# A hybrid diffusion layer on one Trainium2 core: the order of the input projection, its modulation tiles and its recurrent part

## The reference

```
mod = silu(cond) @ w_mod + b_mod          # 6 x 2048: shift, scale, gate for mixer and FFN
h = rmsnorm(x, g0) * (1 + sc_m) + sh_m
u = h @ w_in                              # 5120 columns, 10 blocks of 512
   aq ak av | bx bg | cq ck cv | dq dk dv
o_a = diff_attention(rope(aq), rope(ak), av)        # 4 heads
o_b = scan_fwd + scan_bwd of the gated bx, times gelu(bg)   # recurrent part (RG-LRU), 4 x 128 channels
o_c = neighbourhood attention (context: plain)      # 4 heads
o_d = gqa(rope(rmsnorm(dq)), rope(rmsnorm(dk)), dv) # 4 query heads, 2 key heads
x = x + g_m * rmsnorm([o_a o_b o_c o_d] @ w_out, g1)
x = x + g_f * rmsnorm((silu(g) * a) @ w_ffn_out, g3)
```

## Time and profile before

| | before |
|---|---|
| time, median of 3 | 1951.66 us (1950.04 to 1957.4) |
| the profiled execution: time, span | 1952.1 us, 1950.3 us |
| mean granted TensorE clock | 0.968 |
| PE busy | 1810.2 us (93%), 9305 matmul records |
| PEld busy | 1538.0 us (79%) |
| DVE busy | 828.4 us (42%) |
| ACT busy | 652.4 us (33%) |
| POOL busy | 138.7 us (7%) |
| DMA | 315.20 MB, mean 162 GB/s |

### The profile page before, as it was taken

The page is one execution under the profiler, slowest core; times in us unless marked ns, Lnnn a source line. Parts: engine busy times, 40 slices in busy tenths (PEclk is TensorE's granted clock), DMA queues, the critical chain, the costliest instruction groups (busy, mean ns, idle before and its releaser), DMA issues.

```text
span 1950.3 us, 21901 instructions
## 1 busy us (share of the span) xinstructions
PE 1810.2 (93%) x9305; PEld 1538.0 (79%) x9305; DVE 828.4 (42%) x1156; ACT 652.4 (33%) x915; POOL 138.7 (7%) x224
## 2 busy tenths in 40 slices
PE   5789999999866899599999999999999999999995
PEld 1457767676544788499999999999999988888884
DVE  2323445352575443553333333333333355555553
ACT  1222323243455233332222222222222334444441
POOL 1000023100283000000000000000000000000000
PEclk9899999999889899799999999999999999999998
DMA  9785777877800333133333333333333333333321
GB/s 352 310 317 217 291 296 288 307 296 292 289 1 6 116 121 130 44 129 119 122 128 130 130 130 130 120 121 127 130 130 130 130 108 126 121 122 128 130 87 65
DMA packets 44506, 315.20 MB, mean 162 GB/s; under 512 B 5388, under 2 KB 5768, under 8 KB 7096
## 3 DMA queue, kind: packets, MB, share of 16 engines
q1 hardware_dynamic: 41216, 297.95, 41.4%
q0 software_dynamic: 2864, 12.64, 1.8%
q10 hardware_dynamic: 328, 3.21, 0.5%
HBM read 308.40 MB, written 5.37 MB: 161 GB/s over the span
## 4 chain that ended last, share of the span: by engine, by line
PE 88%; POOL 4%; DVE 3%; DMA 2%; ACT 2%; issue 1%; SPq 0%; DVEq 0%; ACTq 0%; POOLq 0%
PE ps L785 38%; PE ps L580 14%; PE ps L581 14%; PE ps L582 14%; PE ps L555 4%; DMA raw<-in_weights 1%; DVE wlo L846 1%; PE ps L764 1%; POOL pool_t L1220 1%; DMA nabias<-rpb_pad 1%; PE ps L629 1%; DVE x_sb L1139 1%; ACT whi L292 1%; PE ps L607 1%; PE ps L564 0%
## 5 line engine op out<-in xcount | busy, mean ns | idle before, releaser
L846 DVE TENSOR_TENSOR wlo<-raw,whi 128x1024 fp32r<-128x1024 f32 x376 | 458.2, 1230 | 878.1 <-ACT whi L292 877.9
L292 ACT ACTIVATE whi<-raw 128x1024 fp32r<-128x1024 f32 x376 | 392.8, 1058 | 891.0 <-PE ps L785 505.4
L785 PE MATMUL ps<-h_hi,whi 128*128 128x384 f32 x1408 | 471.6, 335 | 0.0
L785 PE MATMUL ps<-h_lo,whi 128*128 128x384 f32 x1408 | 470.5, 334 | 0.0
L785 PE MATMUL ps<-h_hi,wlo 128*128 128x384 f32 x1408 | 470.4, 334 | 0.0
L580 PE MATMUL ps<-whi,h_hi 128*128 128x512 f32 x672 | 275.6, 410 | 18.7 <-DVE wlo L846 17.5
L581 PE MATMUL ps<-whi,h_lo 128*128 128x512 f32 x672 | 266.3, 396 | 0.0
L582 PE MATMUL ps<-wlo,h_hi 128*128 128x512 f32 x672 | 265.7, 395 | 0.0
L785 PEld LDWEIGHTS ps<-h_hi,whi 128*128 128x128 f32 x1408 | 264.5, 188 | 0.1
L785 PEld LDWEIGHTS ps<-h_lo,whi 128*128 128x128 f32 x1408 | 264.5, 188 | 0.0
L785 PEld LDWEIGHTS ps<-h_hi,wlo 128*128 128x128 f32 x1408 | 264.5, 188 | 0.0
(11 more groups left out here) (207 smaller groups left out, 1141.9 us busy)
## 6 DMA issues: line engine op xcount, KB each, us to landing
raw<-in_weights SPq DMA_DIRECT2D x284, 1024.0 KB, 4.9
xT<-in_x_t ACTq DMA_DIRECT2D x1, 3072.0 KB, 11.7
out<-x_sb POOLq DMA_DIRECT2D x3, 1024.0 KB, 4.7
x_sb<-in_x_sample POOLq DMA_DIRECT2D x1, 2048.0 KB, 9.6
gw<-in_lru_gate_w POOLq DMA_DIRECT2D x4, 256.0 KB, 7.5
out<-U POOLq DMA_DIRECT2D x4, 256.0 KB, 9.2
nabias<-rpb_pad POOLq DMA_DIRECT2D x16, 64.0 KB, 9.5
x_sb<-in_x_prompt POOLq DMA_DIRECT2D x1, 1024.0 KB, 5.3
```

The source lines that it names most:

```text
L292: nc.scalar.activation(whi[:, 2 * (g % RING) + b], raw[:, t % RAW, HK * b:HK * b + HK].rearrange("p k n -> p (k n)"), ACT.Copy).then_inc(w ...
L785: return nc.tensor.matmul(ps[bank][:, 0:T], w[:, k % KH * P:(k % KH + 1) * P], xs[:, k, :], start=first, stop=last)
L846: V.tensor_tensor(wlo[:, 2 * (t % RAW) + b], raw[:, t % RAW, HK * b:HK * b + HK].rearrange("p k n -> p (k n)"), whi[:, 2 * (g % RING) + b] ...
```

## The change

The blocks of the projection get another order (BX, BG, DQ, DK and DV, then AQ, AK, AV, CQ, CK, CV). Its 40 tiles become 40 steps, each with two modulation tiles ahead of one projection tile. In the first 16 steps the first four blocks take turns, one K part (four k) each; every part is a sum of its own in PSUM (bank sets 0 to 2 and 4 to 6 by turns), written to U by ACT for the first part (`part_out`) and added to U by DVE for the other three (`part_add`). From step 16 on a block's four tiles are summed in banks 0 to 2 and copied by `u_out`. Modulation uses bank 3 (and 7 for odd m below 8); m = 22 and 23 come after the last step. Within a projection tile the token block is the outer loop, and mod_turn stands behind the first token block. The recurrent part uses banks 4 to 7, begins after step 15, takes three steps per group, and PE transposes straight out of U, so the two POOL copies go. U is stored as [partition, block, token block, 512]. The input h is formed in xT instead of xnT. On POOL the norm of dq and dk moves behind the gelu of group 0, their rope behind that of group 1, and the rope of heads A behind group 3.

```diff
 def in_step(s):
+    return (s % EARLY, s // EARLY) if s < EARLY * KG else (s // KG, s % KG)
 def tile_plan():
-    for g in range(1, 4):
-        for part in range(2):
-            plan += [("mod", 2 * g + part, kg) for kg in range(KG)] + [("in", part, g - 1)]
-    plan += [("in", n, 3) for n in range(2)]
-    for e in range(N_EL):
-        m = 8 + 2 * e
-        for kg in range(KG):
-            plan += [("in", 2 + e, kg), ("mod", m + kg // 2, 2 * (kg % 2)), ("mod", m + kg // 2, 2 * (kg % 2) + 1)]
+    for s in range(STEPS):
+        m, half = 2 + s // 2, s % 2
+        plan += [("mod", m, 2 * half), ("mod", m, 2 * half + 1), ("in",) + in_step(s)]
+    plan += [("mod", m, kg) for m in (22, 23) for kg in range(KG)]
...
 # ACT
+            for s in range(STEPS):
+                if s % 2:
+                    rows_out(2 + s // 2)
+                if s + 1 < STEPS:
+                    hi("in", *in_step(s + 1))
+                if s == EARLY * KG:
+                    act.wait_ge(l_setup, 2)
+                if s < EARLY:
+                    part_out(s)
+                elif s >= EARLY * KG and s % KG == 0 and s // KG > EARLY:
+                    u_out(s // KG - 1)
+                if s % 4 == 3 and s < 12:
+                    h_high(range(s + 1, s + 5), 0, xT)
+                if lru and phase == 0:
+                    lru_in(i)          # copies, then wait l_g1(i + 1), tanh of the gelu
+                if lru and phase == 1:
+                    lru_gates(i)
+                if lru and phase == 2:
+                    lru_sqrt(i)
...
 # PE
+            def in_freed(s, tb):
+                if s < EARLY * KG:
+                    e = s - 2
+                    if e < 0:
+                        return
+                    if e < EARLY:
+                        pe.wait_ge(part_a, TB * e + tb + 1)
+                    else:
+                        pe.wait_ge(part_d, TB * (e - EARLY) + tb + 1)
+                elif s == EARLY * KG:
+                    pe.wait_ge(part_d, TB * (s - EARLY) - TB + tb + 1)
+                elif s % KG == 0:
+                    pe.wait_ge(u_done, TB * (s // KG - EARLY - 1) + tb + 1)
...
+            for s in range(STEPS):
+                m, half = 2 + s // 2, s % 2
+                mod_tile(m, 2 * half)
+                mod_tile(m, 2 * half + 1)
+                in_tile(s, m if half else None)
+                i, phase = (s - EARLY * KG + 1) // 3, (s - EARLY * KG + 1) % 3
+                if 0 <= i < 4 and phase == 0:
+                    lru_turn(i)        # i = 0 waits for part_add of steps 13 and 15
+                if 0 <= i < 4 and phase == 1:
+                    lru_gates(i)       # waits l_xp, l_xc, gw_in
+            for m in (22, 23):
+                for kg in range(KG):
+                    mod_tile(m, kg)
                 mod_turn(m)
...
 # DVE
+            for s in range(STEPS):
+                if s + 1 < STEPS:
+                    lo("in", *in_step(s + 1))
+                if lru and phase == 0:
+                    lru_conv(i)
+                if s % 2:
+                    mod_out(2 + s // 2)
+                if s % 4 == 3 and s < 12:
+                    first_h(s // 4 + 1)
+                if EARLY <= s < EARLY * KG:
+                    part_add(s)
+                if lru and phase == 1:
+                    lru_decay(i)
+                if lru and phase == 2:
+                    lru_scan(i)
...
 # POOL
             for n in range(4):
-                if n == 0:
-                    pool.wait_ge(acc_free, 2)
-                else:
-                    pool.wait_ge(l_y, n)
+                if n:
+                    pool.wait_ge(l_gate, 4 * n)
                 pool.dma_start(gw[:, :, :], ...).then_inc(gw_in, 16)
-                G.tensor_copy(AA[0][:, 0:T]..., U[:, :, BX + n * P:BX + (n + 1) * P])
-                G.tensor_copy(AA[1][:, 0:T]..., U[:, :, BG + n * P:BG + (n + 1) * P])
...
+                if n == 0:
+                    pool.wait_ge(part_d, TB * EARLY * (KG - 1))
+                    norm_d(4, DQ, 0, 0)
+                    norm_d(2, DK, 1, 12)
                 if n == 1:
-                    rope(AQ, 8, 16, 64, 128)
-                    rope(AK, 8, 16, 64, 128)
+                    rope(DQ, 6, 32, 192, 320)
...
+            pool.wait_ge(u_done, TB * 2)
+            rope(AQ, 8, 16, 64, 128)
+            rope(AK, 8, 16, 64, 128)
```

More of the change, by code:

```diff
@@ L350, in _ @@
[L350 to L366, removed]
@@ L509, in _ @@
             squares(4)
-            h_high(range(KD), KD)
+            h_high(range(KD), KD, xnT)
             for f in range(FK):
@@ new lines, in in_tile @@
+            def in_tile(s, mid=None):
+                n, kg = in_step(s)
+                t = TILE[("in", n, kg)]
+                parts = list(halves(t))
+                first = s < EARLY * KG or kg == 0
+                last = s < EARLY * KG or kg == KG - 1
+                pe.wait_ge(h_ls, KG * kg + KG)
+                for tb in range(TB):
+                    in_freed(s, tb)
+                    xs = slice(tb * P, (tb + 1) * P)
+                    acc = ps[in_bank(s, tb)][:, :]
+                    for b, wh, wl in parts:
+                        for kk in range(HK):
+                            k = KG * kg + HK * b + kk
+                            cols = slice(kk * NC, (kk + 1) * NC)
+                            begin, end = first and b == 0 and kk == 0, last and b == 1 and kk == HK - 1
+                            nc.tensor.matmul(acc, h_hi[:, k, xs], wh[:, cols], start=begin, stop=False)
+                            nc.tensor.matmul(acc, h_lo[:, k, xs], wh[:, cols], start=False, stop=False)
+                            ins = nc.tensor.matmul(acc, h_hi[:, k, xs], wl[:, cols], start=False, stop=end)
+                        if tb == TB - 1:
+                            ins.then_inc(w_used, 1)
+                    if last and tb < TB - 1:
+                        ins.then_inc(acc_ps, 1)
+                    if tb == 0 and mid is not None:
+                        mod_turn(mid)
@@ L618, in _ @@
             pe.wait_ge(par_cp, 2)
-            for g in range(1, 4):
-                for part in range(2):
-                    for kg in range(KG):
-                        mod_tile(2 * g + part, kg)
-                    h_tile("in", part, g - 1, ready=0, mid=2 * g + part)
-            for part in range(2):
-                h_tile("in", part, 3, ready=0)
-            def gate(g):
-                d, kind = g % 2, g // 2
-                nc.tensor.matmul(ps[g % 3][:, 0:LW], gw[:, 2 * d + kind, :], XC[:, 0:LW], start=True, stop=True)\
-                    .then_inc(l_gate, 1)
@@ new lines, in lru_gates @@
+            def lru_gates(i):
+                pe.wait_ge(l_xp, i + 1)
+                pe.wait_ge(l_xc, i + 1)
+                pe.wait_ge(gw_in, i * 16 + 16)
+                for g in range(4):
+                    d, kind = g % 2, g // 2
+                    nc.tensor.matmul(ps[4 + g][:, 0:LW], gw[:, 2 * d + kind, :], XC[:, 0:LW], start=True, stop=True)\
+                        .then_inc(l_gate, 1)
+            for s in range(STEPS):
[8 more added lines that the diff above has]
+                    lru_gates(i)
@@ new lines, in part_add @@
+            def part_add(s):
+                n, kg = in_step(s)
+                for tb in range(TB):
+                    if tb < TB - 1:
+                        dve.wait_ge(acc_ps, 2 * ENDS[s] + tb + 1)
+                    else:
+                        dve.wait_ge(w_used, used("in", n, kg))
+                    if kg == 1:
+                        dve.wait_ge(part_a, TB * n + tb + 1)
+                    else:
+                        dve.wait_ge(part_d, TB * (s - 2 * EARLY) + tb + 1)
+                    V.tensor_tensor(U[:, n, tb, :], U[:, n, tb, :], ps[in_bank(s, tb)][:, :], ALU.add).then_inc(part_d, 1)
@@ L1018, in _ @@
+            mod_out(22)
             mod_out(23)
@@ L1378, in weight_tiles @@
         elif kind == "in":
-            out[t] = rows(w_in, in_n[a], b)
+            out[t] = rows(w_in, IN_BLOCKS[a], b)
         elif kind == "out":
```

386 lines of the change are left out of this document (170 added, 216 removed).

## The result

| | before | after |
|---|---|---|
| median, us | 1950.85 (1949.69 to 1957.4) | 1992.67 (1986.1 to 1994.47) |
| profiled execution, us | 1952.1 | 1993.21 |
| its span, us | 1950.3 | 1991.4 |
| granted clock, mean | 0.968 | 0.962 |

The ratio is 1.0202, 95% interval 1.0174 to 1.023: the change costs 41.8 us, where the prediction had 15.5 (1967, range 1953 to 1986). The sign was right, the size was not.

A forecast was written before the change was run, and what follows sets the result against it. PE, carrying 88% of the chain, was taken as the bound, so its idle time and clock counted; savings in opening and attention against new waits summed to +15.5 us, giving 1967 against the median, range 1953 to 1986.

The forecast's parts named there:

- GpSimd queue: Norms ahead of group 1's gate weights and gelu make PE wait 12.0 us at lru_gates(1), bounds 7 and 21.
- opening, waits on wlo: In the opening, five PE waits of 2.92 us on the remainder copy wlo go: −14.6 us.
- first_h at steps 3, 7, 11: Early projection: PE waits for input parts, 2.65 us at step 3 and 0.9 each at steps 7 and 11.
- block boundaries: At four block starts from step 24, PE waits 5.5 us each for u_out behind the rounding: +22.0 us.
- end of the projection, idle: Eight modulation tiles come last instead of two, waiting on weight landings: +1.1 us.
- clock, PE busy time: Opening's low clock goes, −6.1 us; five new waits cost 1.6 us each in low clock, +8.0.
- attention: Norms, D rope and bias addition leave it: −8.8 us for four A heads, −3.3 for the head across the rope_ok wait.
- port lock: Rival: norms and wlo take turns on shared DVE/GpSimd ports, norms and gate wait lengthen by about 9 us: 1976; chance 0.17.
- boundaries hidden: Rival: u_out is done before PE's two modulation tiles, so 22.0 and 6.4 us of clock fall away: 1939; chance 0.10.
- GpSimd wait hidden: Rival: norms run fast or start early, so the gate wait of 12 and 1.6 us clock go: 1953; chance 0.10.
- doesn't do what it says: Rival: the opening keeps its waits, 1988; chance 0.06 shared with the low clock rival.
- low clock for whole tiles: Rival: whole tiles run slow after each of five waits, 6.6 us more each: 2000; chance 0.06 shared with kept opening waits.

The follow-up runs named there:

- e1: The changed kernel with ACT's U copies put ahead of the modulation row copies and the rounding at block boundaries; 1964.6 us, ratio 1.0062.
- e2: The changed kernel with the norms and rope of dq and dk moved behind group 3 of the gate loop on GpSimd; 1978.86 us, ratio 1.0141.
- e5: The changed kernel with U copies first on ACT and the norms and rope of D behind group 3 on GpSimd; 1945.06 us, ratio 0.9967.
- e9: The kernel before, rounding first in the opening, D column blocks early, their norms and rope behind recurrent stage 1; 1926.94 us, ratio 0.9875.
- e4: The changed kernel with the norms and rope of D put back into the attention, behind the bias addition; 1980.28 us, ratio 1.0132.
- e6: On top of e5, mod_out and first_h go ahead of lo on DVE, h_high ahead of part_out on ACT; 1938.52 us, ratio 0.9927.
- e7: e5 without the two norm_d calls, leaving out the RMS norm of dq and dk; 1943.92 us, ratio 0.9959.
- e10: e6 with the eight last modulation tiles spread three to a step over steps 32 to 39; 1941.56 us, ratio 0.9947.

## Why the prediction was right in sign and wrong in size

The loss went past the range because three parts of the sum were too small: the GpSimd queue (12.0, measured 19.3), the clock (+1.9, measured +9.8) and small waits put at nothing or too low (8.1 more). Step by step, in us; measured from the waits of after and before, and from the windows:

| step | predicted | measured | off |
|---|---|---|---|
| opening, waits on wlo | −14.6 | 4.4 − 17.5 = −13.1 | +1.5 |
| first_h at steps 3, 7, 11 | +4.45 | 6.4 | +2.0 |
| block boundaries | +22.0 | 22.6 | +0.6 |
| GpSimd queue | +12.0 | 19.3 | +7.3 |
| l_xc, "issue" at L705 | 0 | 2.4 | +2.4 |
| modulation columns | 0 | 4.4 − 3.4 = 1.0 | +1.0 |
| last part_add (L695) | +0.75 | 0.9 | +0.2 |
| end of the projection, idle | +1.1 | 6.4 − 4.3 = 2.1 | +1.0 |
| clock, PE busy time | −6.1 + 8.0 | +9.8 | +7.9 |
| attention | −12.1 | −13.6 | −1.5 |
| ahead of 52.5 us | 0 | +2.0 | +2.0 |

The column on the right adds up to 24.4, of 25.6 (41.1 between the spans less 15.5).

**Right.** The opening lost five of its six waits. The boundaries came as worked out, four times; chain of after at one, in the order that the prediction gave (weights land at 4.89, whi, first copy):

```profile
355.60 4.89 DMA raw<-in_weights
...
361.48 1.04 ACT whi L316
362.52 0.49 ACT U L343
...
363.14 0.77 PE ps L646
```

The Trainium skill (TensorE: Matmul & The Clock Gate, "HAM oscillation — how this bites in real kernels") reports one kernel in which PSUM double-buffering gave no further gain. Here the single bank set cost four waits where two sets had none, and e1 got 28.1 us back with the single set, by the order on ACT. So either is enough: a second bank set, or nothing slow ahead of the copy.

The attention came out near what was said, by another split: an A head takes 8.1 us (585.43 to 617.85 for four), below the 8.9 taken, so the four give 12.1 us where 8.8 was forecast and 10.8 was the bound; the head across the old wait gives 2.3 of 3.3, the C heads lose 1.2, and part of the whole is the clock. That the totals agree within 1.5 is partly luck. Timeline of DVE in after, against the earlier trace rows:

```profile
585.43 0.35 DVE L1119 SCALAR_TENSOR_TENSOR prob<-prob,smalls,prob 128x128 f32<-128x128 f32 x1
...
617.85 0.29 DVE L1123 TENSOR_SCALAR prob<-prob,smalls 128x128 f32<-128x128 f32 x1
```

**Wrong: the size of the GpSimd term.** The step "it takes 42.25 us" took the norms from a stretch in which DVE's instructions are small. In after they run from 250.44 to 299.8; timeline of POOL, against the earlier trace rows:

```profile
250.44 1.04 POOL L1291 TENSOR_TENSOR pool_t<-U 128x512 f32<-128x512 f32 x1
...
299.11 0.72 POOL L1297 TENSOR_TENSOR U<-U,gbc 128x256 f32<-128x256 f32 x1
300.13 0.86 POOL L1329 DMA_DIRECT2D gw<-in_lru_gate_w  x1 [0.29 <-POOL U L1297]
```

That is 49.7 us to the DMA's issue, 7.4 more than taken, which is the miss of the wait. The rest of the step was right: the norms began 13.5 us after step 15 (13 said), PE reached the gates 47.3 us after it (47.2 said), and the landing took 3.35 us. The wait itself lies within its bounds of 7 to 21, the norms beyond their 5. The largest group of POOL's instructions (busy us, mean ns), first after, 250 to 301, then before, 540.5 to 583:

```profile
L1276 POOL TENSOR_TENSOR pool_t<-pool_t 128x128 f32<-128x128 f32 (+6 forms) x36 | 16.8, 466 | 2.8
```

```profile
L1220 POOL TENSOR_TENSOR pool_t<-pool_t 128x128 f32<-128x128 f32 (+6 forms) x36 | 12.2, 338 | 2.8
```

The same instructions take longer beside the projection's DVE work: 50.4 us in e2, 51.6 in e5 and 49.8 in e9, against 42.4 in e4's attention (566.23 to 608.62), as before the change. The rival "port lock" said this, with +9 for the norms. It was the right mechanism about the right size, given a chance of 0.17, and it should have been in the sum: the row for it was read and set aside. The Trainium skill (SBUF — State Buffer, "SBUF: two separate sides") puts it as an exclusive lock on the shared ports, held for a whole instruction. The trace agrees: both engines get longer, each by parts of the other's instructions (the pair of rows at 257.69 and 258.83 in the last section).

**Wrong: the clock.** The five waits at 1.6 were read from waits of 2.9 us. Behind the long wait the eight gate matmuls themselves ran slow, 5.09 us, where the earlier trace rows have 2.15 for six; chain of after:

```profile
303.61 5.09 PE ps L705 x8
```

And the rows shown above hold twenty waits, not five. 9.8 us of busy time were added where 1.9 had been forecast. The shares can be read from the experiments, by TensorE's busy time up to the first scores (2296 to 2298 matmuls): 461.7 in after, 452.1 in e1 without the waits on U, 460.2 in e2 without the gate wait, and 450.6 in e5 without both. So four waits of 5.65 cost 9.6, which is 2.4 each and not 1.6, and the one of 19.3 costs 1.5. The step that failed is the 1.6, taken from a wait half as long. Without both groups of waits the busy time is only 1.3 below before's 451.9, so the 6.1 forecast for the opening were largely taken back by the small waits; this last was not isolated.

**Wrong: small waits left out.** 8.1 us in sum (the table's lines on first_h, l_xc, columns, part_add, wlo and the end). For two of them, h_lo and the modulation columns, e6 shows a cause: on an in-order queue the 2.4 us of `lo` stand ahead of small work that PE needs sooner. For l_xc the cause stays open (3.7 us in e6). At the end, the transfer of the last weight tile began when two of the eight modulation tiles were worked off, and took 9.09; PE had worked off seven by then and waited 2.6. Chain of after:

```profile
562.28 9.09 DMA raw<-in_weights
...
571.42 1.98 PE ps L584 x8
```

Of the rivals, "boundaries hidden", "GpSimd wait hidden" and "doesn't do what it says" are out by the waits; "low clock for whole tiles" had the total nearest (2000) but for a reason that the window doesn't show: 9.8 us more of busy time, and not 1.9 + 33.

## What to carry to other kernels

Before a stage is rebuilt to lose a wait, read which instruction stands ahead of the late one on its engine: exchanging two pairs of lines gave 20 us here, and the rebuilt stage with its new queue order cost 42. When work moves to another place, take its duration from a stretch with the same work beside it on the other engine, and treat each instruction queued behind it as moved as well. Try two repairs together as well as alone: the norms' move gave 13.8 alone and 19.5 with the U copies first.

## What the runs showed of the hardware

- GpSimd and DVE lengthen each other in bits as small as one addition of 8 elements per partition. In after the second of two operations on modulation columns is 1.04 us long beside a multiplication on GpSimd, where such a one takes 0.18 on the chain near the end of the projection:

```profile
575.45 0.18 DVE modc L941
```

The pair beside GpSimd:

```profile
258.61 0.18 DVE L939 TENSOR_REDUCE modc<-ps 128x8 f32<-128x32 f32 x1
258.83 1.04 DVE L941 TENSOR_TENSOR modc<-modc,pc 128x8 f32<-128x8 f32 x1
```

```profile
257.69 2.16 POOL L1297 TENSOR_TENSOR U<-U,gbc 128x512 f32<-128x512 f32 x1
```

The addition ends at 259.87 and the multiplication at 259.85: the addition stood until the other engine's instruction was through. The reduction just ahead of it, which reads PSUM, took its 0.18 us beside the same multiplication.

- The weight remainder is 1218 to 1227 ns without GpSimd beside it and up to 2068 with the norms (tile wlo on DVE, 250 to 301 us of after, against the earlier trace rows; up to 3314 in e5):

```profile
L894 DVE TENSOR_TENSOR wlo<-raw,whi x6: 1226/1308/2068, 255.5 to 282.2; 128x1024 fp32r<-128x1024 f32 x6
```

- The attention's clock is not settled by GpSimd's presence alone: 0.86 in after, 0.82 in before, e4 and e9, 0.81 to 0.84 in e1, e2, e5, e6, e7 and e10, with waits of the same kind. What sets it stays open.
